# The second RMS norm split over the stage before it and the stage after it

## What is computed

```python
def rms_norm(u, g):
    uf = u.astype(jnp.float32)
    return (uf * lax.rsqrt(jnp.mean(jnp.square(uf), -1, keepdims=True) + RMS_EPS) * g).astype(u.dtype)
...
h = layer_norm(ALPHA * x + mix @ w_out) + sigmoid(that @ w_gate) * rms_norm(p @ w_ple)
x = rms_norm(h, gain) + shift          # gain and shift per channel, from the modulation
proj = x @ w_in                        # the projections of the second block
```

## Time and profile before

| | |
|---|---|
| median of 3 runs | 5408.47 us (5407.17 to 5415.03) |
| the profiled execution | 5424.27 us, its span 5422.4 us |
| TensorE busy | 4823.0 us, 89% |
| VectorE busy | 2746.6 us, 51% |
| ScalarE busy | 1086.2 us, 20% |
| mean granted TensorE clock | 0.932 |

### The profile page before, as it was taken

How to read it: one execution, slowest core, us unless ns; L and a number is a source line. 1 busy time by engine, 2 the same in 40 slices (tenths; PEclk the granted TensorE clock), 3 DMA queues, 4 the chain that set the end, 5 groups by cost and what they waited for, 6 DMA issues and landing times. The chain is left out here.

```text
span 5422.4 us, 88614 instructions
## 1 busy us (share of the span) xinstructions
PE 4823.0 (89%) x38270; PEld 3700.7 (68%) x38270; DVE 2746.6 (51%) x3660; ACT 1086.2 (20%) x1497; POOL 721.9 (13%) x658
## 2 busy tenths in 40 slices
PE   9996997999799999674867969999988999999999
PEld 7776887899577767343436747765654557788887
DVE  5776543444445887374664566232464225443342
ACT  2443221222312231000011221111221122110000
POOL 0002331112000362000000011012000000231340
PEclk9998998999898999786888989999998999999999
DMA  3443203111122334524213134136202004212213
GB/s 138 156 157 121 59 27 123 58 58 58 60 89 79 123 140 177 186 78 136 72 72 139 64 134 147 58 104 177 60 24 55 8 5 160 92 49 88 68 44 104
DMA packets 246228, 508.14 MB, mean 94 GB/s; under 512 B 35223, under 2 KB 118488, under 8 KB 245204
## 3 DMA queue, kind: packets, MB, share of 16 engines
q1 hardware_dynamic: 183940, 359.78, 20.6%
q0 software_dynamic: 33392, 117.54, 6.4%
q10 hardware_dynamic: 28512, 25.17, 1.4%
HBM read 349.18 MB, written 150.74 MB: 92 GB/s over the span
## 5 line engine op out<-in xcount | busy, mean ns | idle before, releaser
L4835 PE MATMUL tail_product<-tail_x_hi,tail_w_hi 128*128 128x512 f32 x832 | 329.4, 396 | 11.0 <-DVE tail_x_lo L146 10.8
L4835 PE MATMUL tail_product<-tail_x_lo,tail_w_hi 128*128 128x512 f32 x832 | 325.2, 391 | 0.0
L4835 PE MATMUL tail_product<-tail_x_hi,tail_w_lo 128*128 128x512 f32 x832 | 324.6, 390 | 0.0
L3552 PE MATMUL win_product<-kept_hn_hi,win_w_hi 128*128 128x512 f32 x560 | 229.2, 409 | 39.8 <-DVE win_w_lo L146 39.8
L1758 PE MATMUL front_product<-kept_x_hi,front_w_hi 128*128 128x512 f32 x544 | 220.9, 406 | 10.2 <-DVE kept_x_lo L146 10.0
L3552 PE MATMUL win_product<-kept_hn_lo,win_w_hi 128*128 128x512 f32 x560 | 220.3, 393 | 0.0
L3552 PE MATMUL win_product<-kept_hn_hi,win_w_lo 128*128 128x512 f32 x560 | 220.3, 393 | 0.0
L2751 PE MATMUL oproj_product<-kept_mix_hi,oproj_w_hi 128*128 128x512 f32 x512 | 206.0, 402 | 9.2 <-DVE kept_mix_lo L146 8.6
L1758 PE MATMUL front_product<-kept_x_hi,front_w_lo 128*128 128x512 f32 x544 | 213.9, 393 | 0.0
L1758 PE MATMUL front_product<-kept_x_lo,front_w_hi 128*128 128x512 f32 x544 | 213.4, 392 | 0.0
L3213 PE MATMUL lc_ps<-idft,lc_zz 128*128 128x256 f32 x512 | 121.2, 402 | 90.9 <-DVE lc_zz L3091 90.9
(11 more groups left out here) (741 smaller groups left out, 11235.2 us busy)
## 6 DMA issues: line engine op xcount, KB each, us to landing
s_decayed<-front_ring SPq DMA_DIRECT2D x96, 256.0 KB, 3.9
tail_w<-in_w_gu SPq DMA_DIRECT2D x44, 512.0 KB, 3.3
win_w<-in_w_in SPq DMA_DIRECT2D x35, 512.0 KB, 3.7
front_w<-in_even_w SPq DMA_DIRECT2D x34, 512.0 KB, 3.9
s_pm<-kept_held SPq DMA_DIRECT2D x64, 256.0 KB, 2.0
win_cq_hi_plain<-in_ada_w POOLq DMA_DIRECT2D x16, 1024.0 KB, 5.4
oproj_ring<-in_odd_w POOLq DMA_DIRECT2D x30, 512.0 KB, 3.8
dn_kv<-s_qkv SPq DMA_DIRECT2D x16, 768.0 KB, 6.9
```

The lines of the kernel that those rows point to most:

```text
L3552: mm = pe.matmul(pp[:, u, h, :], l, b, start=(k == 0 and m == 0), stop=(k == depth(s) - 1 and m == 2))
L4835: mm = pe.matmul(pp[:, s % 2, h_, :], l, b, start=(k == 0 and m == 0), stop=(k == deep(s) - 1 and m == 2))
```

## The change

The stage `norm` between the blocks is gone. Its work is split:

- Memory that outlives the stages, `SecondNorm`: h itself (its eight tiles), the identity, gain and bias, the inverse root (128x8), the raw first weight tile, and `hn`, the two split parts. The block end writes h there and uses `hn` for its own split operands.
- In the block end, ScalarE squares each tile of h after it is written, and VectorE adds the squares up, from the third turn on, one tile behind. After the last product TensorE takes the column sums (eight 128x1 matmuls), and a root and a reciprocal on 128x8 give the inverse. SyncE loads the first weight tile and gain and bias behind the fifth store of h. The stage no longer waits for the stores.
- In the projections TensorE first spreads the inverse with eight matmuls. VectorE multiplies each tile of h in place with the gain and the inverse, ScalarE makes the high part with the bias, VectorE the low part. Slot 0 waits for each tile's low part in turn. The clearing of two tiles and the split of weight tile 1 come after the eight tiles. VectorE waits for the stores of h before it overwrites h.

```diff
+class SecondNorm:
+    def __init__(self, nc, gains, first_w):
+        self.ctx = ExitStack()
+        sb = lambda name, *shape: self.ctx.enter_context(nc.sbuf_tensor(f"second_{name}", list(shape), F32))
+        self.h, self.ident, self.gain = sb("h", P, 8, T), sb("ident", P, P), sb("gain", P, 2, 8)
+        self.inv, self.raw = sb("inv", P, 8), sb("raw", P, 8, P)
...
+        self.hn = Kept(nc, "hn", 8, split=True)
...
 def projections, SyncE
                     sp.wait_ge(lower_done, n)
+                    if n == 0:
+                        return
...
                 sp.wait_ge(mod_stored, 32)
+                sp.wait_ge(ahead.stored, 128)
...
 TensorE
+                for b in range(8):
+                    mm = pe.matmul(pb[:, b // 4, b % 4 * P:(b % 4 + 1) * P], ahead.inv[:, b:b + 1].to_broadcast([P, P]), ident[:, :],
+                                   start=True, stop=True)
+                mm.then_inc(inv_spread, 1)
                 for s, (kind, i) in enumerate(SLOTS):
...
                             beside(s, k)
+                            if s == 0:
+                                pe.wait_ge(lower_x, k + 1)
...
 ScalarE
+                act.wait_ge(ahead.gain_in, 32)
+                for k in range(8):
+                    act.wait_ge(turned, k + 1)
+                    act.activation(hn.hi[:, k, :].bitcast(F32R), ahead.h[:, k, :], ACT.Identity, bias=ahead.gain[:, 1, k:k + 1]
+                                   ).then_inc(upper_x, 1)
...
 VectorE
+                def lower_h(k):
+                    dve.wait_ge(upper_x, k + 1)
+                    dve.scalar_tensor_tensor(hn.lo[:, k, :].bitcast(F32R), ahead.h[:, k, :], ahead.gain[:, 1, k:k + 1], hn.hi[:, k, :],
+                                             ALU.add, ALU.subtract).then_inc(lower_x, 1)
+
                 divide(0)
+                dve.wait_ge(ahead.gain_in, 32)
+                dve.wait_ge(ahead.stored, 128)
+                dve.wait_ge(inv_spread, 1)
+                for k in range(8):
+                    dve.scalar_tensor_tensor(ahead.h[:, k, :], ahead.h[:, k, :], ahead.gain[:, 0, k:k + 1], flat(pb), ALU.mult,
+                                             ALU.mult).then_inc(turned, 1)
+                    if k >= 1:
+                        lower_h(k - 1)
+                lower_h(7)
                 dve.memset(xs[:, :], 0.0).then_inc(zeroed, 1)
...
 def second_block
-    hn = Kept(nc, "hn", 8, split=True)
-    norm(nc, "n1", h, 8, hn, None, None, RMS_EPS, c["avg1024"], gains=(mod[:, 48:56], mod[:, 0:8]))
...
 def block_end, SyncE
+                    elif ahead and m == 4:
+                        sp.dma_start(ahead.raw[:, :, :], ahead.first_w).then_inc(ahead.w_in, 16)
+                        for j in range(2):
+                            sp.dma_start(ahead.gain[:, j, :], ahead.gains[j]).then_inc(ahead.gain_in, 16)
-                if not after:
-                    sp.wait_ge(stored, 128)
...
 TensorE
+                if ahead:
+                    pe.wait_ge(h_summed, KT - 1)
+                    for b in range(8):
+                        mm = pe.matmul(ln_cols[:, b:b + 1], side[:, 0, b * P:(b + 1) * P], avg[:, 0:1], start=(b == 0), stop=(b == 7))
+                    mm.then_inc(h_total, 1)
...
 ScalarE
                     act.activation(sq[:, m % 2, :], flat(ps[:, m % 2, :, :]), ACT.Sigmoid).then_inc(gate, 1)
+                    if ahead:
+                        act.wait_ge(h_ready, m + 1)
+                        act.wait_ge(h_summed, max(m - 1, 0))
+                        act.activation(side[:, 1 if m else 0, :], e[:, m, :], ACT.Square).then_inc(h_squared, 1)
+                if ahead:
+                    act.wait_ge(h_root, 1)
+                    act.activation(small[:, 0:8], small[:, 0:8], ACT.Sqrt).then_inc(h_root, 1)
...
 VectorE
+                def add_h(m):
+                    dve.wait_ge(h_squared, m + 1)
+                    dve.wait_ge(h_summed, m - 1)
+                    dve.tensor_tensor(side[:, 0, :], side[:, 0, :], side[:, 1, :], ALU.add).then_inc(h_summed, 1)
...
                     if 18 + m in PG:
                         divide(18 + m)
+                    if ahead and m >= 2:
+                        add_h(m - 1)
+                if ahead:
+                    add_h(7)
+                    dve.wait_ge(h_total, 1)
+                    dve.tensor_scalar(small[:, 0:8], ln_cols[:, 0:8], RMS_EPS, None, ALU.add).then_inc(h_root, 1)
+                    dve.wait_ge(h_root, 2)
+                    dve.reciprocal(ahead.inv[:, :], small[:, 0:8]).then_inc(h_inv, 1)
+                    dve.wait_ge(h_inv, 1)
```

More of the change, by code:

```diff
@@ L118, in free @@
     def free(self):
+        self.ctx.close()
+class SecondNorm:
[4 more added lines that the diff above has]
+        self.inv, self.raw = sb("inv", P, 8), sb("raw", P, 8, P)
+        self.gain_in, self.w_in, self.stored = (nc.alloc_semaphore(name=f"second_{n}") for n in ("gain_in", "w_in", "stored"))
+        self.gains, self.first_w = gains, first_w
+        self.hn = Kept(nc, "hn", 8, split=True)
+    def free(self):
+        self.hn.free()
         self.ctx.close()
@@ L3330, in prep_constants, with projections @@
     return {"prep_sum": w, "prep_spread": s}
-def projections(nc, tag, hn, a, c, mod, rope, outs):
+def projections(nc, tag, ahead, a, c, mod, rope, outs):
     SLOTS = prep_slots()
@@ L3635, in divide @@
                     flat_ = lambda t: t.rearrange("p k m -> p (k m)")
-                    dve.wait_ge(w_in, 16 * (n + 1))
+                    if n == 0:
+                        dve.wait_ge(ahead.w_in, 16)
+                    else:
+                        dve.wait_ge(w_in, 16 * n)
                     if n >= 2:
@@ L5208, in build @@
     mod, rope = dram("mod", P, 64), dram("rope", 4, P, T)
-    h = first_block(nc, a, c, dram, mod, rope)
-    second_block(nc, a, c, dram, h, mod, rope, out)
+    h, ahead = first_block(nc, a, c, dram, mod, rope)
+    second_block(nc, a, c, dram, h, ahead, mod, rope, out)
 def first_block(nc, a, c, dram, mod, rope):
@@ L5237, in first_block, with block_end @@
     mix = hyena_block(nc, a, c, dram, xv, gate, pm, inv_norm)
-    return block_end(nc, a, c, dram, 1, h, mix)
-def block_end(nc, a, c, dram, n, x, mix, held=None, after=None):
+    ahead = SecondNorm(nc, (mod[:, 48:56], mod[:, 0:8]), a["w_in2"][8])
+    return block_end(nc, a, c, dram, 1, h, mix, ahead=ahead), ahead
+def block_end(nc, a, c, dram, n, x, mix, held=None, after=None, ahead=None):
     KT = 8
@@ L5257, in block_end @@
         else:
-            hi = st.sb("hi", [P, KT, T])
-            e_sq, lo = st.sb2("lo", [P, KT, T])
+            hi, lo, e_sq = ahead.hn.hi, ahead.hn.lo, ahead.hn.lo_plain
         if held:
@@ L5263, in block_end @@
         else:
-            res, e = (st.sb(m, [P, KT, T]) for m in ("res", "e"))
+            res, e = st.sb("res", [P, KT, T]), ahead.h
             side, sq, acc = st.sb("side", [P, 2, T]), st.sb("sq", [P, 2, T]), st.sb("acc", [P, T])
@@ L5275, in block_end @@
         w_in, side_in = (st.sem2(m) for m in ("w_in", "side_in"))
-        stored = after.stored if after else st.sem("stored")
+        stored = (after or ahead).stored
+        h_squared, h_summed, h_total, h_root, h_inv = (st.sem(m) for m in ("h_squared", "h_summed", "h_total", "h_root", "h_inv"))
         (w_upper, w_lower, upper_x, lower_x, upper_p, lower_p, prod, wo_out, summed, mean_done, centred, y_squared, e_squared, y_added,
```

20 lines of the change are left out of this document (10 added, 10 removed).

## The result

| | before | changed |
|---|---|---|
| median of 16 runs each | 5423.01 us (5407.17 to 5435.44) | 5391.22 us (5373.49 to 5402.06) |
| ratio | | 0.9935 [0.9925, 0.9946] |
| the profiled execution's span | 5422.4 us | 5377.3 us |

The change gains 31.8 us, 0.65%. The forecast was a gain of 41.5 us and a time of 5367.0 us; the measured time is 24.2 us above it, outside the range of 5358 to 5377. Two things are in these 24.2 us. The base was the median of the first three runs, 5408.47; over 16 runs the same kernel stands at 5423.01, which is 14.5 more. And the gain is 9.7 us smaller than forecast.

The account below looks back on a forecast made before the run. The bound was TensorE's idle interval from the last block-end product to slot 1, 82.8 us. Gain 43.05 - 1.5 = 41.5 us: 5424.27 to 5382.8, less 15.8 gives 5367.0 us, range 5358 to 5377.

Parts of the forecast that it names:

- nothing of it reaches TensorE: Block end's loop: the added Square (1.06 us) and addition (1.23) per turn stay hidden under a 10.88 us product; no cost.
- I carry the difference over whole: Base: the profiled 5424.27 us less the runs' median 5408.47, 15.8 us, subtracted from 5382.8 to give 5367.0.
- The sign of being wrong that I had named: Block end's loop: the forecast is wrong if turns grow beyond 10.9 us.
- The tail: Block end after the last tile of h: additions, sums, root chain and stage end, from 3115.79 to 3123.9 us.
- The column sums: Block end's tail: sixteen TensorE passes, 2.28 us at the lower clock, taken as 2.55 with the first load.
- The projections up to slot 1: Projections' entry: spread 4.2 us, tiles 2.39 us each, then clearing and split; slot 1's start moves 43.05 us earlier.
- rival of a full clock: Tail, spread and new wait: TensorE keeps its full clock; gain 45.3 us, 5363 us; chance 0.2.
- no overlap: Projections: slot 0 starts only after all eight tiles; gain 35 us, 5373 us; chance 0.03.
- GpSimd drawing out the split: Before slot 1: GpSimd's product lengthens VectorE's split by 2.4 us; with slot 0 staying slow as alternative, gain 38 to 40, chance 0.12.
- Slots 1 to 9: Projections after the entry: VectorE starts its bound stretch from slot 2 as before; nothing given back, by 1.4 us.
- bound of 3.1 us for late weights: Projections, slots 2 to 9: upper bound of +3.1 us on the time if weights come late.
- the rival's own 4.5: Weight tile 2 5.9 us later, so VectorE starts slot 2's work up to 4.5 us late; gain 37, chance 0.1.

Follow-up runs that it names:

- pad_before: Kernel before, with an unused tile of 32 bytes per partition ahead of the second block end's split weights: 5421.0 us in one run.
- pad416: Changed kernel with an unused tile of 416 bytes ahead of the second block end's split weights: 5389.08 us, ratio 0.9934.
- pad416_first: Kernel before, with an unused tile of 416 bytes ahead of the first block end's split weights: 5419.42 us in one run.
- whole: Changed kernel, but slot 0 of the projections waits for all eight low parts instead of one at a time: 5388.7 us in one run.
- fill: Changed kernel with four unused matmuls behind each of six of nine sets of column sums, in both block ends: 5399.23 us, ratio 0.9952.

## Why the prediction was wrong

Two steps failed. The one that takes the time out of the range is the base, "I carry the difference over whole": 14.5 of the 24.2 us. On the base of 5423.01 the same forecast would be 5381.5 and its range some 5372.5 to 5391.5, with the measured 5391.22 at its very edge. The one that failed in the kernel is "nothing of it reaches TensorE" in the block end: it cost 4.6 us of a gain that came out 9.7 short. Step by step, in the order of the prediction:

- *Block end, in the loop: "nothing of it reaches TensorE".* This is the step that failed in the kernel. The Squares and additions are hidden indeed, and no idle time appears in the loop. But something was not on my list of what an edit can do: it moves tiles in memory. The high part now lies in the kept `hn` and the weights elsewhere, so their distance modulo 512 went from 0 to 96, and the 720 matmuls of `WO` and the last seven products became slower by about 3%. That costs 2.1 + 2.5 = 4.6 us. pad_before and pad416 show it in both directions. The sign of being wrong that I had named came true: a turn is now 11.25 us (the last tile of h starts at 3107.61, the one ahead of it at 3096.36), where it was 10.88 and I had set 10.9 as the limit.
- *The norms of that stage* I took over unchanged, without a word. In the changed profile they take 42.3 us instead of 37.2, 5.1 more, with 23.9 us at 1.2 GHz instead of 13.6. Whether that belongs to the change is open. For it: all four profiles of the changed kernel with its own layout have 42.3. Against it: three of the kernel before have 37.2, 37.2 and 45.3, and pad416_first, whose edit is in another stage, has 45.3; two changed kernels with a gap tile have 37.3 and 37.4; and the first block end, with nothing changed in it, goes from 37.5 to 45.5. It would take some ten profiles of each kernel to settle it.
- *The tail:* right within 0.9 us. The column sums were mis-sized, 3.58 us for 2.55, and by a wrong reading: I took the 2.28 us of the earlier trace rows as the price at the lower clock, but that row has a mean clock of 0.80. Sixteen passes at 0.50 throughout, right behind other work, take 3.41 us in the changed profile. So the clock is most of the miss, and the 7.29 us of idle time ahead of the sums cost at most the 0.17 between 3.41 and 3.58. Before, then changed:

```profile
3018.57:3020.85 2.28, 2.28 (x18) 2.28 (x17) 2.28 (x3) 0.97 (x1) 0.00 (x0) 0.80 0.47 111
...
2993.64:2997.05 3.41, 3.41 (x18) 3.41 (x17) 2.74 (x3) 1.39 (x2) 0.00 (x0) 0.50 0.01 2
```

- *The projections up to slot 1:* right. The spread, the groups of 2.39 us, the clearing and the split behind them all stand where the sum put them. The rival of a full clock fell, as did that of no overlap (whole shows what it would have looked like) and that of GpSimd drawing out the split. The clock cost 1.7 us in slot 1 (1.5).
- *Slots 1 to 9:* nothing was given back. From slot 2 to the first spread it is 90.0 us in both profiles, and the wait there is 0.8 us (the forecast: under 1). The bound of 3.1 us for late weights had the slack of 1.4 taken off twice; the rival's own 4.5 is 5.9 less 1.4.
- *"I carry the difference over whole":* the largest term of the miss, 14.5 us. The executions of one kernel lie over 28 us apart, and the time mostly goes with the mean granted clock (of the changed kernel, 5373.49 at 0.937 and 5379.05 at 0.936 against 5400.97 at 0.932). Three runs that happened to lie low gave the base, and the profiled execution, 5424.27, was the one nearer to the middle of all. It stood 15.8 us above the median of three, and I read that as its error, while it was the sample's. An allowance of 4 us for a median of three, out of a range of 8 us among them, was too small.

The account of the gain: 42.3 at the seam, less 1.7 in slot 1, less 4.6 by the pace, gives 36.0 us; with the 5.1 of the norms taken off too it gives 30.9. The medians differ by 31.8, but that the second sum comes nearer doesn't show that the norms belong. The interval of the ratio stands for 29 to 41 us and holds both sums, and the two profiles from which they are read differ by 45.1 us in all, 8.3 of them by the first block end.

A rival for the missing microseconds lies behind the seam, and no experiment was aimed at it. From slot 2 to the end the six profiles with the norm's stage take 2206 to 2215 us (mean 2212), the nine without it 2207 to 2227 (mean 2219). The difference lies mainly in two later stages whose code and places are the same, and the longer profiles have more time at 1.2 GHz behind slot 2 (152 us of it in the shortest, 200 in the longest). Whether that is chance or follows from the change is open.

## What to carry to other kernels

A change that moves tiles to other memory touches every product that reads them: compare the count of matmuls in a stretch of equal length, before and after, at equal granted clock, ahead of any theory on engines. Where several runs of one kernel lie 0.5% apart, read a gain of 0.7% stage by stage from two traces, and set the range of a forecast by the scatter of runs rather than by the few that are shown. A cover found for work (here 2 us of waiting for the spread) is best filled by what comes last in the queue otherwise: moving the clearing there gave 3.8 us at the seam and in slot 1. And when a price is taken from a row, take the granted clock of that very row with it.

## What the hardware showed

- The pace of back-to-back 128x512 matmuls (fp32r) at full clock depends on where the two operands lie relative to each other. Mean spacing by the distance modulo 512: 0: 226.6 to 227.2 ns in every stage measured that has it, the projections of both kernels among them; 32: 233.3; 96: 234.2; 128: 232.5 to 233.3; 160: 233.3. All that were tried other than 0 are slower by some 3%. Moving the weights by 32 bytes is enough (pad_before). The remainder of each alone isn't it: in the projections both operands lie at 0 in the kernel before and at 96 in the changed one, and both have 226.6. The mechanism isn't shown; distances of 256 or more, other shapes and other types were not tried.
- The granted clock among the norms of one stage is not the same in each execution. Unchanged code had 13.6 us at 1.2 GHz there in two profiles and 30.7 in a third, 8.1 us apart in time. Ahead of each of these falls stand column sums of 128x1, small matmuls, though not every set of them is followed by a fall; four larger matmuls put behind six of the sets did not prevent them (fill).
- Sixteen passes of 128x1 sums take 1.84 us at a granted clock of 1.00 and 3.41 at 0.50, right behind other work.
- The same VectorE cast took 0.67 us alone and 2.85 when it started 0.13 us behind a GpSimd product. The subtraction that had started 1.02 us ahead of that product kept its 1.23 us.
